# The front projection of a hybrid decoder layer in two passes, with pairs of tiles as seven block products

## The reference

```
h = layer_norm(x, ln0_g, ln0_b)
proj = einsum('btd,dc->btc', h, w_in)          # 2048 x 1024 by 1024 x 4096
qa, ka, va, qb, kb, vb, gate = split(proj)
ya = dilated_mixture(qa, ka, va, rel_bias);  yb = stick_breaking(qb, kb, vb)
out = (concat(ya, yb) * silu(gate)) @ w_out + b_out
return layer_norm(ALPHA * h + out, ln_g, ln_b)
```

## Time and profile before

| | |
|---|---|
| median of 3 runs | 1634.42 us (1634.22 to 1635.87) |
| profiled execution | 1635.06 us, its span 1633.3 us |
| TensorE matmul, busy | 1598.9 us, 98% |
| VectorE, busy | 1112.2 us, 68% |
| ScalarE, busy | 727.5 us, 45% |
| GpSimd, busy | 382.1 us, 23% |
| first matmul of the opening stretch | 18.59 us |
| first matmul of the rest of the front phase | 106.10 us |
| first matmul of an "a" tile (stick phase) | 493.35 us |
| first score of the dilated phase | 1140.17 us |

### The profile page before, as it was taken

How to read it: one execution, slowest core, us unless ns; L and a number is a source line. 1 busy time by engine, 2 the same in 40 slices (tenths; PEclk the granted TensorE clock), 3 DMA queues, 4 the chain that set the end, 5 groups by cost and what they waited for, 6 DMA issues and landing times.

```text
span 1633.3 us, 26457 instructions
## 1 busy us (share of the span) xinstructions
PE 1598.9 (98%) x9102; PEld 1376.3 (84%) x9102; DVE 1112.2 (68%) x2188; ACT 727.5 (45%) x1788; POOL 382.1 (23%) x236
## 2 busy tenths in 40 slices
PE   5999999999999999999999999999999999999997
PEld 4777888888888888888888888887999999987886
DVE  5731124322227888888888888888678787878888
ACT  5541113201224555555555555555677667641000
POOL 2200000000000111111111111012577778761232
PEclk9999999999999999999999999999999999999999
DMA  5434666645659564945485548532667777465542
GB/s 182 154 120 117 219 232 229 209 145 170 217 198 283 181 197 147 285 161 181 164 270 168 181 153 236 165 127 77 192 157 205 191 203 197 137 204 187 166 153 78
DMA packets 183052, 295.55 MB, mean 181 GB/s; under 512 B 51801, under 2 KB 108500, under 8 KB 178132
## 3 DMA queue, kind: packets, MB, share of 16 engines
q1 hardware_dynamic: 180756, 294.01, 58.1%
q10 hardware_dynamic: 2080, 0.01, 0.1%
q0 software_dynamic: 96, 0.04, 0.0%
HBM read 185.66 MB, written 104.01 MB: 177 GB/s over the span
## 4 chain that ended last, share of the span: by engine, by line
PE 88%; DVE 4%; DMA 3%; SPq 1%; POOL 1%; issue 1%; ACT 1%; DVEq 0%; ACTq 0%; POOLq 0%
PE proj L385 25%; PE proj_a L1074 16%; PE out_ps L1898 7%; PE wt_ps L1043 7%; PE oa_ps L1461 6%; PE z_ps L1033 4%; PE o_ps L1059 4%; PE z_ps L1032 4%; PE o_ps L1057 4%; PE pt_ps L1442 3%; PE s_ps L1433 3%; PE s_ps L1434 2%; SPq L1351 1%; DMA b_col<-in_ln_b 1%; PE vtp L407 1%
## 5 line engine op out<-in xcount | busy, mean ns | idle before, releaser
L1097 ACT ACTIVATE z_ps<-z_ps 128x512 f32<-128x512 f32 (+2 forms) x320 | 165.8, 518 | 277.1 <-PE z_ps L1033 276.9
L1152 DVE TENSOR_TENSOR_SCAN W<-z_ps,W,zeros 128x512 f32<-128x512 f32 x192 | 245.8, 1280 | 55.4 <-ACT z_ps L1097 55.0
L385 PE MATMUL proj<-h_hi,w_hi 128*128 128x512 f32 x608 | 243.9, 401 | 4.9 <-DVE h_lo L565 3.7
L385 PE MATMUL proj<-h_hi,w_lo 128*128 128x512 f32 x608 | 238.0, 391 | 0.0
L385 PE MATMUL proj<-h_lo,w_hi 128*128 128x512 f32 x608 | 237.4, 390 | 0.0
L1495 ACT ACTIVATE prob<-neg_s,rows 128x256 f32<-128x256 f32 (+1 forms) x384 | 173.6, 453 | 89.7 <-DVE rows L1542 89.0
L1160 DVE TENSOR_TENSOR WT_lo<-wt_ps,WT_hi 128x512 fp32r<-128x512 f32 (+1 forms) x320 | 187.7, 587 | 5.9 <-ACT WT_hi L1105 5.9
L1105 ACT ACTIVATE WT_hi<-wt_ps 128x512 fp32r<-128x512 f32 (+1 forms) x320 | 169.9, 531 | 10.8 <-PE wt_ps L1043 9.3
L1043 PE MATMUL wt_ps<-ident,W 128*128 128x128 f32 x1088 | 171.9, 273 | 0.1
L1542 DVE CUSTOM_DVE_ANT_0 neg_s<-s_ps,h_lo 128x256 f32<-128x256 f32 (+1 forms) x384 | 122.9, 363 | 63.9 <-PE s_ps L1434 54.5
L1011 POOL TENSOR_TENSOR y_sum<-y_sum,ends 64x512 f32<-64x512 f32 x32 | 33.1, 1033 | 565.0 <-DVE y_sum L1167 565.0
(11 more groups left out here) (196 smaller groups left out, 3136.1 us busy)
## 6 DMA issues: line engine op xcount, KB each, us to landing
wa_hi<-wa_d SPq DMA_DIRECT2D x48, 512.0 KB, 3.7
wa_lo<-wa_d SPq DMA_DIRECT2D x48, 512.0 KB, 4.8
wa_d<-x_sb SPq DMA_DIRECT2D x24, 512.0 KB, 3.7
va_d<-st SPq DMA_DIRECT2D x48, 256.0 KB, 2.7
va<-va_d SPq DMA_DIRECT2D x12, 1024.0 KB, 8.5
w_raw<-in_w_tiles SPq DMA_DIRECT2D x18, 512.0 KB, 5.0
x_sb<-in_x SPq DMA_DIRECT2D x16, 512.0 KB, 5.5
qk_hi_d<-st SPq DMA_DIRECT2D x32, 256.0 KB, 2.6
```

The lines of the kernel that those rows point to most:

```text
L385: last = pe.matmul(acc_of(n)[:], w[w_slot(t)][:, k, :], h[ch][:, k, :], start=(k, a) == (0, 0), stop=(k, a) == (KD - 1, 2))
L1097: act.activation(z_ps[n % Z_SLOTS][:, 0:width], z_ps[n % Z_SLOTS][:, 0:width], ACT.Sigmoid, scale=-SCALE).then_inc(w_done, 1)
L1152: dve.tensor_tensor_scan(W[n % W_SLOTS][:, 0:width][:, ::-1], z_ps[n % Z_SLOTS][:, 0:width][:, ::-1], above[:, ::-1], first, ALU.mult, ALU ...
```

## The change

The front phase makes its twenty tiles in two passes, of chunks 0 and 1 and of chunks 2 and 3. A pass opens with four lead tiles in 16 steps, of 12 matmuls and four transposes each. The other sixteen tiles go in eight pairs. A pair of tiles (a, b) and a pair of chunks form a product of 2 x 2 blocks, where the weights' blocks are A11, A12 (tile a, first and second half of K) and A21, A22 (tile b), and h's are B11, B21 (even chunk, first and second half of K) and B12, B22 (odd chunk). Its eight block products are replaced by seven, of 12 matmuls each (Strassen's scheme in Winograd's form):

- weight sums, GpSimd (`weigh`), four for each pair and pass: S1 = A21+A22, S2 = S1-A11, S3 = A11-A21, S4 = A12-S2;
- h sums, once for each pass and half-K slice: T1 = B12-B11, T3 = B22-B12 on GpSimd (`t13`), T2 = B22-T1, T4 = B21-T2 on VectorE (`t24`), and each is split in high (ScalarE) and low (VectorE) into the buffers that held chunks 2 and 3 before, during steps 10 to 15 and just behind;
- products A11 B11, S2 T2, A12 B21, S1 T1, S3 T3, S4 B22, A22 T4, in four PSUM banks in turn;
- result sums, VectorE (`combine`), seven for each pair and pass, into SBUF tiles F (the first product is copied there by ScalarE). The results are evicted from F, not from PSUM.

ScalarE now writes the scaled h to an SBUF tile `full`, from which the high and low parts are taken; before it stayed in PSUM. Each pair's seven half-K weight blocks are split apart, into a ring of nine slots. The raw tiles of a pair have one buffer. Chunk 2's x tiles are loaded in the last two pairs of the first pass and its first two steps made behind product 5 of the last pair. h's chunks 0 and 1 are stored and loaded back now; `stick_phase` takes the chunks in the order 2, 3, 0, 1.

The twelve "a" weight tiles are no longer split and stored beforehand. In `stick_phase` SP loads each raw tile (`wa_raw`, one buffer) and GpSimd makes both parts (`split_wa`), 48 times, between its `y_sum` operations; TensorE waits for the split. The first loads of the dilated phase come in 20 DMAs of one chunk, before in 10.

```diff
@@ front_phase: constants and order @@
-    GROUPS = [(t, ch) for ch in range(NCH) for t in range(LEAD)]
-    GROUPS += [(t, ch) for t in range(LEAD, W_TILES) for ch in range(NCH)]
+HALF = KD // 2
+PASSES = 2
+LEAD = 4
+PAIRS = (W_TILES - LEAD) // 2
+PRODUCTS = 7
+RING = 9
+SUMS = 7
+    A11, S2, A12, S1, S3, S4, A22 = range(PRODUCTS)
+    OPERAND = ((0, 0), (2, HALF), (0, HALF), (2, 0), (3, 0), (1, HALF), (3, HALF))
+    T2_, T1_, T3_, T4_ = range(4)
+    U2, SUM11, U4, U3, SUM22, SUM12, SUM21 = range(SUMS)
+    T_PLACE = ((2, HALF), (2, 0), (3, 0), (3, HALF))
+    T_OF = {1: T2_, 3: T1_, 4: T3_, 6: T4_}
+    RESULTS = []
+    for p in range(PASSES):
+RESULTS += [(t, 2 * p) for t in range(LEAD)] + [(t, 2 * p + 1) for t in range(LEAD)]
+for i in range(PAIRS):
+    a, b = LEAD + 2 * i, LEAD + 2 * i + 1
+    RESULTS += [(a, 2 * p), (a, 2 * p + 1), (b, 2 * p), (b, 2 * p + 1)]
+    KIND = [TILES[t][0] for t, _ in RESULTS]
+    PER_PASS = 2 * LEAD + 4 * PAIRS
...
+    FIRST_ORDER = (A11, S2, A12, A22, S1, S3, S4)
+    ORDER = (A11, A12, A22, S2, S1, S3, S4)
...
@@ SyncE @@
+    def load_raw(i):
+        for t in range(2):
+            sp.dma_start(raw[t], w_tiles[LEAD + 2 * i + t]).then_inc(raw_loaded, 16)
...
+                if r == 6 and i + 2 < PAIRS:
+                    sp.wait_ge(s_done, 4 * (PAIRS * p + i + 2))
+                    sp.wait_ge(w_split, block_split(p, i + 1, A22))
+                    load_raw(i + 2)
...
+                    if i == PAIRS - 2 and r == 6:
+                        sp.wait_ge(w_split, block_split(0, PAIRS - 1, A22))
+                        load_x(2 * QB)
+                        load_x(2 * QB + 1)
+                    if i == PAIRS - 1 and r == 2:
+                        sp.wait_ge(w_split, block_split(0, PAIRS - 1, S4))
+                        load_x(2 * QB + 2)
+                        load_x(2 * QB + 3)
...
@@ GpSimd @@
+    def t13(p, j):
+        b11, b22, b12 = full[0][:, j, :], full[0][:, HALF + j, :], full[1][:, j, :]
+        pool.wait_ge(full_done, STEPS * p + KD + 2 * j + 1)
+        pool.wait_ge(lo_done, STEPS * p + KD + 2 * j + 1)
+        pool.tensor_tensor(b11, b12, b11, ALU.subtract).then_inc(t13_done, 1)
+        pool.wait_ge(full_done, STEPS * p + KD + 2 * j + 2)
+        pool.wait_ge(t13_done, 2 * (HALF * p + j) + 1)
+        pool.tensor_tensor(b12, b22, b12, ALU.subtract).then_inc(t13_done, 1)
+    def weigh(p, i):
+        s = 4 * (PAIRS * p + i)
+        flat = [tile.rearrange("p k c -> p (k c)") for tile in raw]
+        a11, a12, a21, a22 = flat[0][:, 0:CH], flat[0][:, CH:D], flat[1][:, 0:CH], flat[1][:, CH:D]
+        pool.wait_ge(raw_loaded, 32 * (PAIRS * p + i + 1))
+        if i > 0:
+            pool.wait_ge(w_split, block_split(p, i - 1, S4))
+        pool.tensor_tensor(sums[S1], a21, a22, ALU.add).then_inc(s_done, 1)
+        pool.wait_ge(s_done, s + 1)
+        pool.tensor_tensor(sums[S2], sums[S1], a11, ALU.subtract).then_inc(s_done, 1)
+        pool.tensor_tensor(sums[S3], a11, a21, ALU.subtract).then_inc(s_done, 1)
+        pool.wait_ge(s_done, s + 2)
+        pool.tensor_tensor(sums[S4], a12, sums[S2], ALU.subtract).then_inc(s_done, 1)
...
+        t13(p, 0)
+        t13(p, 1)
+        weigh(p, 0)
+        t13(p, 2)
+        t13(p, 3)
+        for i in range(1, PAIRS):
+            weigh(p, i)
...
@@ TensorE @@
+    def lead_bank(p, chunk, t):
+        if chunk == 0 and p > 0:
+            if t < 2:
+                pe.wait_ge(second_done, V_RESULTS[len(V_RESULTS) // PASSES * p - 1] + 1)
+            else:
+                pe.wait_ge(sum_done, summed(p - 1, PAIRS - 1, SUM22 if t == 2 else SUM12))
+        if chunk == 1:
+            if t >= 2:
+                pe.wait_ge(second_done, early(p, 0, t - 2) + 1)
+            elif p > 0:
+                pe.wait_ge(sum_done, summed(p - 1, PAIRS - 1, (SUM21, U4)[t]))
+    def lead(p, s):
+        chunk, k = s // KD, K_OF[s]
+        pe.wait_ge(lo_done, STEPS * p + s + 1)
+        for t in range(LEAD):
+            if s == 0:
+                pe.wait_ge(w_split, lead_split(p, t))
+            if s % KD == 0:
+                lead_bank(p, chunk, t)
+            wk = slot_of(p, 2 * t + k // HALF) * HALF + k % HALF
...
+    def product_bank(p, i, r):
+        if i == 0 and r < 4:
+            pe.wait_ge(second_done, early(p, r // 2, 2 + r if r < 2 else r - 2) + 1)
+        elif r < 4:
+            pe.wait_ge(sum_done, summed(p, i - 1, (SUM22, SUM12, SUM21, U4)[r]))
+        elif r == 4:
+            pe.wait_ge(p1_copied, PAIRS * p + i + 1)
+        else:
+            pe.wait_ge(sum_done, summed(p, i, U2 if r == 5 else SUM11))
+    def product(p, i, r):
+        pe.wait_ge(w_split, block_split(p, i, r))
+        product_bank(p, i, r)
+        h, first_k = OPERAND[r]
+        bank, ws = acc[r % 4], slot_of(p, 2 * LEAD + PRODUCTS * i + r) * HALF
+        for j in range(HALF):
+            if i == 0 and r in T_OF:
+                pe.wait_ge(t_lo_done, 4 * (HALF * p + j) + T_OF[r] + 1)
...
+        for i in range(PAIRS):
+            for r in range(PRODUCTS):
+                product(p, i, r)
+                if r == 4 and i in VALUE_PAIRS:
+                    transpose_values(result(p, i, C11))
+                if i - 1 in VALUE_PAIRS and r < 3:
+                    transpose_values(result(p, i - 1, (C12, C21, C22)[r]))
...
+                if p + 1 < PASSES and i == PAIRS - 1 and r == 5:
+                    for s in range(T_SLOTS):
+                        transposes(p + 1, s)
@@ ScalarE @@
-        act.activation(tp[s % T_SLOTS][:], tp[s % T_SLOTS][:], ACT.Identity,
+        whole = full[(k < HALF) == (chunk == 1)][:, k, :]
+        act.activation(whole, tp[s % T_SLOTS][:], ACT.Identity,
                        scale=g_col[:, k:k + 1], bias=b_col[:, k:k + 1]).then_inc(full_done, 1)
...
+            if s == KD + 1:
+                first(early(p, 0, 0))
+                first(early(p, 0, 1))
+            if s == KD + 2:
+                first(early(p, 0, 2))
+            if s == KD + 3:
+                first(early(p, 0, 3))
+            if s == KD + 4:
+                high_block(p, 0, A11)
+            if s >= KD + 2:
+                j, odd = divmod(s - KD - 2, 2)
+                for which in ((T3_, T4_) if odd else (T2_, T1_)):
+                    high_t(p, j, which)
...
@@ VectorE @@
+    def t24(p, j):
+        t1, t2, t4 = full[0][:, j, :], full[0][:, HALF + j, :], full[1][:, HALF + j, :]
+        dve.wait_ge(t13_done, 2 * (HALF * p + j) + 2)
+        dve.wait_ge(lo_done, STEPS * p + KD + 2 * j + 2)
+        dve.tensor_tensor(t2, t2, t1, ALU.subtract).then_inc(t24_done, 1)
+        dve.wait_ge(t24_done, 2 * (HALF * p + j) + 1)
+        dve.tensor_tensor(t4, t4, t2, ALU.subtract).then_inc(t24_done, 1)
...
+    def combine(p, i, what):
+        f11, f21 = f_tile(p, i, C11), f_tile(p, i, C21)
+        f12, f22 = f_tile(p, i, C12), f_tile(p, i, C22)
+        r, before, old, a, new = {U2: (1, None, (2, C21), f11, f21), SUM11: (2, U2, None, f11, f11),
+                                  U4: (3, SUM11, (1, C12), f21, f12), U3: (4, U4, None, f21, f21),
+                                  SUM22: (4, U3, (1, C22), f12, f22), SUM12: (5, SUM22, None, f12, f12),
+                                  SUM21: (6, SUM12, None, f21, f21)}[what]
+        dve.wait_ge(used, made(p, i, r))
+        if what == U2:
+            dve.wait_ge(p1_copied, PAIRS * p + i + 1)
+        else:
+            dve.wait_ge(sum_done, summed(p, i, before))
+        if old is not None and i >= old[0]:
+            dve.wait_ge(second_done, result(p, i - old[0], old[1]) + 1)
+        dve.tensor_tensor(new, acc[r % 4][:], a, ALU.add).then_inc(sum_done, 1)
...
@@ stick_phase @@
+    CHUNKS = (2, 3, 0, 1)
-return kind, row, a // A_TILES
+return kind, row, CHUNKS[a // A_TILES]
     def load_wa(a):
-        if a >= 2:
-            sp.wait_ge(a_done, a - 1)
-        for part, tile in enumerate((wa_hi, wa_lo)):
-            sp.dma_start(tile[a % 2][:].bitcast(F32), wa_d[a % A_TILES, part]).then_inc(wa_loaded[a % 2], 16)
+        if a >= 1:
+            sp.wait_ge(wa_split, a)
+        sp.dma_start(wa_raw[:], w_tiles[W_TILES + a % A_TILES]).then_inc(wa_loaded, 16)
...
+    def split_wa(a):
+        pool.wait_ge(wa_loaded, 16 * (a + 1))
+        if a >= 2:
+            pool.wait_ge(a_done, a - 1)
+        pool.tensor_copy(wa_hi[a % 2][:], wa_raw[:]).then_inc(wa_hi_done, 1)
+        pool.wait_ge(wa_hi_done, a + 1)
+        pool.tensor_tensor(wa_lo[a % 2][:], wa_raw[:], wa_hi[a % 2][:].bitcast(F32),
+                           ALU.subtract).then_inc(wa_split, 1)
+    pool.wait_ge(*front.weights_split)
+    split_wa(0)
+    pool.wait_ge(wa_split, 1)
+    pool.wait_ge(front.used, front.made(PASSES - 1, PAIRS - 1, 5))
     for slot in range(Q_SLOTS):
         pool.memset(q_lo0[slot][DH:P, :].bitcast(F32), 0.0).then_inc(q_zeros_set, 1)
+    pool.wait_ge(q_zeros_set, Q_SLOTS)
+    pool.wait_ge(front.used, front.made(PASSES - 1, PAIRS - 1, PRODUCTS - 1))
+    split_wa(1)
```

(10 more changed lines are left out.)

864 lines of the change are left out of this document (531 added, 333 removed).

## The result

The changed kernel takes 1651.06 us (median of four runs, 1647.54 to 1653.47), the kernel before, on the same chip, 1634.34 (1634.22 to 1635.87): 1.0098 of it, 95% interval 1.0074 to 1.0122. So it is slower by 16.7 us, where 21.4 us less were forecast and the range ended at 1631. The profiled execution took 1653.47 us (span 1651.9) against 1635.06. Of the executions of experiments 5 and 8, one each took far longer than the rest (3146.94 and 1952.67 us) and is left out of their ratios.

A forecast was written before the change was run, and what follows sets the result against it. TensorE's matmuls were taken to bound the kernel, almost nothing waiting. -43.5 - 4.8 + 3.2 + 12.8 + 3.4 + 2.0 + 2.4 + 3.0 = -21.5 us gave 1613 us; range 1597 to 1631.

The forecast's parts named there:

- The matmuls that go: Front phase: 192 fewer matmuls at 0.2267 us each on TensorE, 43.5 us less.
- (a): Step 8 of each pass: TensorE waits 1.6 us for a bank still being read, 3.2 us in all.
- (b): Lead steps making T sums: VectorE and GpSimd take turns at SBUF, holding TensorE 6.4 us a pass, 12.8 in all.
- The rival of a free port: GpSimd's turns fall in gaps, so T steps and pairs cost nothing: 1596 us, chance 0.17.
- (c): Between passes: late normalised x tiles and first h_lo cost 2.6 us, a later x tile 0.8; 3.4 together.
- The 4.8 us of waits of before: TensorE's waits in the old opening order, up to 110 us, go entirely: 4.8 us less.
- (d): Pairs: 2.0 us in the passes' first pairs, 2.4 for late first differences in four "vb" pairs.
- (e): Start of stick phase: first a-weight split late by 0.5 us, second by 2.5; 3.0 together.
- (f): Stick phase: 46 more GpSimd splits, a 10.5 us chain hidden in groups 12.96 us apart; 0 us.
- late splits: Rival for the stick phase: chain of 14 us makes each of 46 groups wait, 48 us, 1661; chance 0.06.
- a rival in which it stays down through the T steps: Low clock in each pass's eight T steps doubles them, 1648 us; chance 0.05.

The follow-up runs named there:

- experiment 5: Changed kernel with a-weight loads sooner, last front-phase stores ahead of loads, and two evictions one step sooner: 1625.27 us, 0.9940 of the kernel before.
- experiment 8: experiment 7 with the first pair's four block sums of each pass also moved from GpSimd to VectorE: 1623.61 us, 0.9939 of the kernel before.
- experiment 3: Changed kernel with the evictions of the even chunk's first two lead tiles one step sooner, both passes: 1641.73 us, 1.0049 of the kernel before.
- experiment 7: experiment 5 with the eight activation differences of a pass moved from GpSimd to VectorE: 1621.23 us, 0.9910 of the kernel before.
- experiment 9: experiment 6 and experiment 7 together, with second and third product's weights split ahead of the last block's T1, T3, T4: 1621.64 us, 0.9923 of the kernel before.
- experiment 12: experiment 7 timed again, beside experiment 11 on the same chip: 1621.70 us, 0.9924 of the kernel before.
- Experiment 11: experiment 7 with the odd chunk's fourth lead tile eviction behind S4's split and the first pair's first-block eviction later: 1625.33 us, 0.9963 of the kernel before.
- experiment 1: Changed kernel with raw a-weight loads, third tile on, planned some 4 steps (8 us) sooner in SyncE's order: 1638.01 us, 1.0027 of the kernel before.
- the best version: The kernel of experiment 7, as timed again in experiment 12: 1621.70 us, 0.9924 of the kernel before.
- made wait: One of ten TensorE waits put on purpose into the kernel before's first projection, behind chains of GpSimd memsets: 1709.40 us, 76.2 more than the kernel before.
- experiment 2: Changed kernel with the projection's three last stores ahead of loads at the start of the stick phase: 1643.61 us, 1.0063 of the kernel before.
- experiment 4: Changed kernel with GpSimd's four first-pair block sums behind all eight activation differences, both passes: 1650.84 us, 1.0107 of the kernel before.
- experiment 6: experiment 5 with no a-projection matmuls dealt to the first two steps of the stick phase: 1624.04 us, 0.9930 of the kernel before.

## Why the prediction was wrong

By the parts of the forecast:

- The matmuls that go, 43.5 us: right. There are 192 fewer, and product groups end 2.72 us apart (VectorE's sums at 479.59, 482.31 and 485.03 us of the changed kernel follow them), in the pairs from 140 to 240 us without a wait.
- (a), the bank: 3.2 us forecast, 3.9 measured. The wait was right and its price was not: taking it away brought the a-tiles 8.5 us forward in the trace, and 8.0 us, known to about 5, in the times (experiment 3).
- (b), the T steps: 12.8 us forecast, and the waits on h_lo there are 12.8. The mechanism, the two engines taking turns, is the right one. The equal number is luck. The unit prices were low (VectorE's operation of 512 columns with two SBUF inputs takes 0.69 alone, not 0.61; GpSimd's 1.29, not 1.19). With the measured ones my own sum makes 8.1 us for a pair of steps and 5.2 for the weight sums, some 9 us a pass and 18 in all (an estimate); against that stands that the two engines overlap in part, a pair of their operations taking about 1.7 us, not 0.69 + 1.29. What I did not draw from it: if each GpSimd operation costs VectorE more than the 0.69 us of doing it itself, it is no help. The traces of experiments 7, 9 and 12 show this for the differences, that of experiment 8 that it does not hold where VectorE has nothing left. The rival of a free port is out. The Trainium skill (SBUF — State Buffer, Who interferes with whom) gave the rule, and the traces agree: 1.44 to 1.78 us beside GpSimd's two-input operations, 0.69 without them, and 0.68 beside them where one input is in PSUM.
- (c), between the passes: 3.4 us forecast, 3.6 measured: 3.4 for x at the pass's first transposes, where 2.6 were forecast, and 0.2 for a later x tile, where 0.8 were.
- The 4.8 us of waits of before, all taken off: wrong by 1.7. That much of them stood ahead of the very first product, behind the first x tile, and stays: the product starts at 18.58 us, before at 18.59.
- (d), the pairs: 4.4 us forecast, 5.0 measured, at another place. None of the "vb" pairs waits for its differences. The two waits are at the end of each pass's first pair, for sums that stand on VectorE behind an eviction that ScalarE could not begin, for want of a staging slot (2.0, 3.1 and 2.8 us of waits for a landing between 91 and 100 us). Experiment 11 showed it.
- (e), the start of the stick phase: 3.0 us forecast, 5.1 measured, and not for the split that I priced but for a store behind fifteen loads. The split was late as well, by about as much (497.62 us), so that taking the store's wait away left 2.4 us of it. (In my sum the first split is ready at 18.9, before TensorE's 19.0, and yet I counted 0.5 for it; no such wait is in the trace.) "The loads' k, q and stores pass on SP in the same order as now" is the sentence that failed: I took the order, and did not ask what the new evictions, one store later than before in their ring, do in it.
- (f), the splits of the stick phase: 0 forecast, 11.2 us in three waits measured, and their clock. This step failed outright: its chain of 10.5 us in a group of 12.96 had "a load of 4.8", which is a median, and nothing for the time until the load is asked for (nor did I price that the first loads of the dilated phase become 20 DMAs instead of 10). At the change of the chunk and of the head, behind 19 other DMAs, that load landed after 9.9 us, and had been asked for 2.7 us after ScalarE began to evict the group before; at the first loads of the dilated phase it was 6.5 and 7.7 us. The first is 7.8 us more than my 4.8, the second 9.4, where the chain had 2.5 to spare. The rival named it (late splits, 0.06) and priced it for all 46 groups at once; it happens at three, and there it is large. "The load is issued before the group ahead has ended" was true at all three, and was no argument: it was not early enough.
- What had no term: the clock, 21.4 us in the profiled execution. A long wait is paid a second time, and some short ones are. I had weighed the clock only as a rival in which it stays down through the T steps, and took its 1.00 in the opening stretch of before as evidence against it, where no wait was longer than 1.7 us.

The sum of the corrections: waits in the front phase 25.9 for 23.8, +2.1; the 1.7 us at the start that stay, +1.7; waits in the stick phase 16.3 for 3.0, +13.3; the clock +21.4. From -21.5 that makes +17.0 us; the profiled executions differ by 18.4. So two terms account for the wrong sign, the late DMAs at four places and the clock behind the waits; without either of them alone the changed kernel would have been within about 4 us of the one before. They are not independent: experiment 1 took late DMAs away, and the clock behind two of them came back with them. That the stick phase as a whole is not slowed by GpSimd's splits was right: its scan takes 1280 ns, as in the earlier trace rows, and with the loads in time no wait is left in it but the one at its start.

Still open: how much of experiment 7's gain over 5 is the clock, and how large it is in the times, since their intervals overlap; what decides whether a short wait is followed by a low clock; and the 9 us between the best version (12.4 us under the kernel before) and the forecast (21.4). Its own waits on h_lo, between the passes and for the sums remain in the trace, with a clock of 0.91 in four stretches of 20 us of the front phase (experiment 7); no run took them away one by one.

## What to carry to other kernels

When work moves from a phase where it was hidden into one where it must arrive in time, read the DMA queue at its worst places, the change of a chunk, a head or a phase, and price the load with what stands ahead of it there, both until it is asked for and until it lands, not with its median. Price a wait of a TensorE-bound kernel twice: its own length, and 1.4 to 2.8 us of lost clock behind it, and don't count on short ones being free of it; here two bank waits of 3.9 us together, moved away, brought the end of the phase 8.5 us forward in the trace. And before GpSimd is given a share of VectorE's work, compare what its operation costs VectorE with what the operation would cost VectorE itself: eight differences a pass moved back made the phase shorter by 5 us in the traces.

## What the runs showed of the hardware

The price of a made wait in clock does not follow its length: 1.4 to 2.8 us behind waits of 4.1 to 9.4 us, 1.7 behind 2.89, 0.1 behind 2.46. The Trainium skill (TensorE: Matmul & The Clock Gate, HAM oscillation — how this bites in real kernels) says of a matmul kernel that waits 3 to 5 us for data between its bursts that each burst starts cold again; the trace agrees for nine of the ten made waits.

Shorter waits go either way, at the same place and for the same length. The wait of 2.5 us for VectorE's sums in the first pass had a clock of 1.00 behind it in the changed kernel (106.6 us) and of 0.57 in experiment 3 (103.1 us; the stretch 104 to 108). The bank wait of 1.97 us had a low clock behind it in the first pass in all four traces that have it (0.65, 0.57, 0.79 and 0.81 from 52 to 56 us, in the changed kernel and experiments 1, 2 and 4), in the second pass only in the changed kernel. The shortest wait with a low clock behind it is the one for the one-hot rows: in the five traces in which it was 0.6 to 4.6 us (the changed kernel and experiments 1, 5, 6 and 11) the clock fell there, in the others, where it was 0.4 us or nothing, it did not. The bias matmuls of 33 rows follow it in all of them.

GpSimd's own operations stretch too when both want SBUF. One of the four block sums of the changed kernel, 14 times from 114 us on (least, median and greatest duration in ns), and the same beside VectorE's T steps in the first pass:

```profile
L479 POOL TENSOR_TENSOR x_sb<-x_sb x14: 1284/1292/1755, 114.4 to 453.1; 128x512 f32<-128x512 f32 x14
...
60.89 1.73 POOL L479 TENSOR_TENSOR x_sb<-x_sb 128x512 f32<-128x512 f32 x1
```

1.29 us is the usual length of the operation, 1.63 to 1.74 that of the five between 60.9 and 69.4 us: neither of the two engines gets its full rate there, though both together take less than one behind the other would (1.7 us for a pair, not 1.98).
